# First branch of a two-layer block: scores with the queries on partitions, both directions in one weight map

## What is computed

```python
dmat = jnp.where(tril, b[..., :, None] - b[..., None, :] + ic[..., None, :], -jnp.inf)
a = jnp.exp(dmat - m_row[..., None]) * jnp.einsum('bhtd,bhsd->bhts', qc, kc)
num = jnp.einsum('bhts,bhsv->bhtv', a, vc) + ...
den = jnp.sum(a, axis=-1) + ...
h = num / jnp.maximum(jnp.abs(den), jnp.exp(-m_row))[..., None]
...
return h_lat[0] + h_lat[1], h_ctx[0] + h_ctx[1]      # forward + backward
...
hn = rmsnorm(h, a_norm_w)                            # then * sigmoid(o) * silu(z)
```

## Time and profile before

| what | value |
|---|---|
| median of 3 runs | 2305.05 us (2304.82 to 2305.26) |
| profiled execution, its own time | 2304.28 us |
| its span, first to last instruction | 2302.1 us |
| PE busy | 2278.4 us, 99% |
| DVE busy | 1335.7 us, 58% |
| ACT busy | 1066.3 us, 46% |
| granted TensorE clock, mean | 0.999 |
| DMA | 294.48 MB, mean 128 GB/s |

### The profile page before, as it was taken

One profiled execution on the slowest core, in us unless ns is written; L12 is line 12 of the kernel. 1 busy time (PEld: TensorE's weight loads), 2 busy tenths in 40 slices (PEclk: granted clock), 3 DMA queues, 4 the chain that ended last, 5 costly groups with the idle time before them and its releaser, 6 DMA issues.

```text
span 2302.1 us, 36859 instructions
## 1 busy us (share of the span) xinstructions
PE 2278.4 (99%) x15426; PEld 2033.1 (88%) x15426; DVE 1335.7 (58%) x2557; ACT 1066.3 (46%) x2064; POOL 237.6 (10%) x248
## 2 busy tenths in 40 slices
PE   8999999999999999999999999999999999999998
PEld 7888878999978998889999999999989888979887
DVE  6544443477754223456455676547667876667875
ACT  5533322355442223354443555445376554476553
POOL 0000000322201012100002221120100110100110
PEclk9999999999999999999999999999999999999999
DMA  7422224221234222233333223446524545323554
GB/s 305 170 75 75 74 110 183 93 74 56 74 108 147 75 74 88 86 130 109 110 129 131 108 77 108 176 140 218 165 93 141 189 168 192 133 82 139 190 178 144
DMA packets 52628, 294.48 MB, mean 128 GB/s; under 512 B 9008, under 2 KB 15408, under 8 KB 21168
## 3 DMA queue, kind: packets, MB, share of 16 engines
q1 hardware_dynamic: 52464, 292.15, 35.4%
HBM read 288.98 MB, written 3.41 MB: 127 GB/s over the span
## 4 chain that ended last, share of the span: by engine, by line
PE 93%; DVE 4%; ACT 2%; DMA 0%; issue 0%; SPq 0%; DVEq 0%; ACTq 0%
PE PS L583 90%; PE PS L587 3%; DVE TM L2339 1%; ACT TM L1625 1%; ACT TMG L1625 1%; DVE wl L2358 0%; DMA raw<-in_wpk 0%; DVE colS L2347 0%; DVE colS L2892 0%; DVE TMG L2347 0%; DVE wl L2360 0%; DVE HY L2347 0%; DVE TM L2508 0%; ACT HY L1625 0%; DVE TM L2347 0%
## 5 line engine op out<-in xcount | busy, mean ns | idle before, releaser
L583 PE MATMUL PS<-HY,wh 128*128 128x512 f32 (+3 forms) x4944 | 1278.1, 342 | 3.4 <-DVE HY L2347 1.0
L583 PEld LDWEIGHTS PS<-HY,wh 128*128 128x128 f32 (+2 forms) x4944 | 848.2, 189 | 115.6 <-issue 4.1
L583 PE MATMUL PS<-HY,wl 128*128 128x256 f32 (+1 forms) x3000 | 926.1, 309 | 0.0
L2358 DVE TENSOR_TENSOR wl<-raw,wh 128x1280 fp32r<-128x1280 f32 (+3 forms) x241 | 350.5, 1454 | 429.0 <-ACT wh L1635 428.8
L583 PEld LDWEIGHTS PS<-HY,wl 128*128 128x128 f32 x3000 | 567.4, 189 | 30.0
L583 PE MATMUL PS<-wh,HY 128*128 128x256 f32 x2916 | 551.7, 286 | 0.2
L583 PEld LDWEIGHTS PS<-wh,HY 128*128 128x128 f32 x2916 | 461.8, 191 | 3.4 <-ACT TM L1625 1.6
L1625 ACT ACTIVATE TM<-PS 128x512 f32<-128x512 f32 (+5 forms) x383 | 190.1, 510 | 584.1 <-PE PS L583 473.8
L583 PE MATMUL PS<-wl,HY 128*128 128x256 f32 x1458 | 412.5, 283 | 0.0
L1635 ACT ACTIVATE wh<-raw 128x1280 fp32r<-128x1280 f32 (+2 forms) x247 | 297.1, 1203 | 217.5 <-PE PS L583 138.7
L583 PEld LDWEIGHTS PS<-wl,HY 128*128 128x128 f32 x1458 | 279.4, 192 | 0.4
(11 more groups left out here) (190 smaller groups left out, 1693.1 us busy)
## 6 DMA issues: line engine op xcount, KB each, us to landing
raw<-in_wpk SPq DMA_DIRECT2D x233, 1024.0 KB, 4.8
raw<-in_wpk SPq DMA_DIRECT2D x32, 704.0 KB, 4.0
TM<-in_wpk SPq DMA_DIRECT2D x6, 1024.0 KB, 16.3
X<-in_xin SPq DMA_DIRECT2D x1, 2048.0 KB, 15.7
Y<-in_wpk SPq DMA_DIRECT2D x2, 1024.0 KB, 20.4
Y<-bias_d SPq DMA_DIRECT2D x4, 512.0 KB, 10.3
raw<-in_wpk SPq DMA_DIRECT2D x3, 512.0 KB, 3.7
T<-in_tabs SPq DMA_DIRECT2D x1, 1216.0 KB, 5.5
```

The source lines that it names most:

```text
L583: return P.x.matmul(o, l, r, start=start, stop=stop)
L2358: D.x.tensor_tensor(wl[:, s, 0:c], raw[:, r, 0:c], wh[:, s, 0:c], ALU.subtract).then_inc(*lo_split.mark((u, 0)))
```

## The change

The scores are computed with the queries on partitions. DVE multiplies scores and weights and sums each row in the same instruction (`tensor_tensor_reduce`), so the column of ones goes. The denominators of all tiles and both directions are worked out together, each direction's map is scaled by its reciprocal, and both are added into one map `a_w`. PE turns this map with transposes (`turns`), ACT copies it to SBUF (`a_wt`, in the buffer `Y`), and PE multiplies it by the values once (`outs`). ACT squares and scales straight from PSUM. Where these steps stand: for heads 1 to 3 `turns` is between the two passes of `a_z`; for head 0 of layer 0 it is after them; for head 0 of layer 1 the next head's queries (`queries(1)`) come first. `used("a_o")` on ACT and DVE moves ahead of the exponentials and products in head 0, and behind `a_w` on DVE in the others.

```diff
+        a_valid = ({i: (0, 128 * i + 128) for i in range(4)}, {0: (0, 256), 1: (128, 256), 2: (0, 512), 3: (0, 512)})
+        a_masks = (mb, mf)
+        a_diagonals = [TM[:, o:o + 2560].rearrange("p (i c) -> p i c", c=640)[:, :, 0:128] for o in (2052, 4100)]
+        a_w = (a_b[:, 0, 0:256], a_f[:, 1, 0:256], a_b[:, 2], a_f[:, 3])
+        a_den = colS[:, 8:16].rearrange("p (d i) -> p d i", d=2)
...
+        def a_turn_bank(i):
+
+            return bank(4)[:, 256 * i:256 * i + 256] if i < 2 else bank(4 + i)
...
+        def a_out_bank(l, i):
+
+            if l:
+                return bank(i)[:, 0:256]
+            return bank(2 + i // 2)[:, 256 * (i % 2):256 * (i % 2) + 256]
...
+                def turns(h):
+                    for i in range(i0, 4):
+                        P.wait_ge(dve_step, ("a_w", l, h, i))
+                        for k in range(0, a_keys(i), 128):
+                            t = turned(a_turn_bank(i)[:, k:k + 128], a_w[i][:, k:k + 128])
+                        if i:
+                            t.then_inc(*pe_step.mark(("a_turned", l, h, i)))
+
+                def outs(h):
+                    P.wait_ge(act_step, ("a_v", l, h, 1))
+                    for i in range(i0, 4):
+                        P.wait_ge(act_step, ("a_wt", l, h, i))
+                        last = a_keys(i) // 128 - 1
+                        for j in range(last + 1):
+                            t = mm(a_out_bank(l, i), a_wt(i)[:, 128 * j:128 * j + 128], a_v[:, j], j == 0, j == last)
+                        if l:
+                            t.then_inc(*pe_step.mark(("a_out", l, h, i)))
+                        elif i % 2:
+                            t.then_inc(*pe_step.mark(("a_out", l, h, i - 1), ("a_out", l, h, i)))
...
                     if h:
-                        P.wait_ge(dve_step, ("a_h", l, h - 1, 3))
+                        P.wait_ge(act_step, ("a_hn", l, h - 1))
                     for d in range(2):
-                        t = mm(bank(2 + d)[:, t0:512], ident[dirs[d], 32 * d + h:32 * d + h + 1].to_broadcast([4, 128]), a_r[d][:, t0:512])
+                        t = mm(bank(2 + d), ident[dirs[d], 32 * d + h:32 * d + h + 1].to_broadcast([4, 128]), a_c[d])
...
+                    for i in range(i0, 4):
+                        n = a_keys(i)
+                        mm(bank(4 + i)[:, 0:n], a_qk[:, 0, 128 * i:128 * i + 128], a_qk[:, 1, 0:n]).then_inc(
+                            *pe_step.mark(("a_s", l, h, i)))
...
+                        if h and c == 0:
+                            turns(h)
+                    if h:
+                        outs(h)
+                        if h < 3:
+                            queries(h + 1)
+                            keys(h + 1)
+                    elif l == 0:
+                        turns(0)
+                        queries(1)
+                        outs(0)
+                        keys(1)
+                    else:
+                        queries(1)
+                        turns(0)
+                        keys(1)
+                        outs(0)
...
+                def turned_weights(h):
...
+                    if l == 0:
+                        A.wait_ge(pe_step, ("a_turned", l, h, 1))
+                        act(Yf[:, 0:512], bank(4), ACT.Copy, ("a_wt", l, h, 0), ("a_wt", l, h, 1))
+                    for i in range(2, 4):
+                        A.wait_ge(pe_step, ("a_turned", l, h, i))
+                        act(a_wt(i), a_turn_bank(i), ACT.Copy, ("a_wt", l, h, i))
+
+                def squares_of(h):
+                    if h:
+                        A.wait_ge(pe_step, ("a_yt", l, h - 1, 1))
+                    for i in range(t0 // 128, 4):
+                        A.wait_ge(pe_step, ("a_out", l, h, i))
+                        act(a_h[:, i], a_out_bank(l, i), ACT.Square, ("a_sq", l, h), scale=0.5, accum_out=colS[:, 24 + i:25 + i])
...
+                    A.wait_ge(dve_step, ("a_root", l, h))
+                    for i in range(t0 // 128, 4):
+                        act(a_h[:, i], a_out_bank(l, i), ACT.Copy, ("a_hn", l, h), scale=colS[:, 28 + i:29 + i])
+
                 for h in range(4):
+                    if h == 0:
+                        used("a_o", 4 * l)
...
+                        x = a_diagonals[d][:, t0 // 128:4]
+                        act(x, x, ACT.Exp, *[("a_ex", l, h, d, i) for i in range(t0 // 128, 4)])
...
-                    used("a_o", 4 * l + h)
+                        used("a_o", 4 * l + h)
...
+                        if h and c == 0:
+                            turned_weights(h)
+                    if h:
+                        used("a_z", 4 * l + h)
+                        squares_of(h)
+                        scaled(h)
+                        if h < 3:
+                            queries(h + 1)
+                            keys(h + 1)
+                    elif l == 0:
+                        turned_weights(0)
+                        used("a_z", 0)
+                        queries(1)
+                        squares_of(0)
+                        scaled(0)
+                        keys(1)
+                    else:
+                        used("a_z", 4)
+                        queries(1)
+                        turned_weights(0)
+                        keys(1)
+                        squares_of(0)
+                        scaled(0)
...
-                        D.wait_ge(pe_step, ("a_out", l, h - 1, 3))
+                        D.wait_ge(pe_step, ("a_turned", l, h - 1, 3))
...
-                    for j in range(4):
-                        D.wait_ge(pe_step, ("a_s", l, h, j))
-                        for d in range(2):
-                            for a, z in a_valid[d][j]:
-                                a = max(a, t0)
-                                if z > a:
-                                    D.wait_ge(act_step, ("a_ex", l, h, d, j))
-                                    tt(a_dirs[d][:, j, a:z], bank(4 + j)[:, a:z], a_dirs[d][:, j, a:z], ALU.mult, ("a_at", l, h))
-                    used("a_o", 4 * l + h)
+                    if h == 0:
+                        used("a_o", 4 * l)
+                    for d in range(2):
+                        for i in range(i0, 4):
+                            a, z = a_valid[d][i]
+                            D.wait_ge(pe_step, ("a_s", l, h, i))
+                            D.wait_ge(act_step, ("a_ex", l, h, d, i))
+                            D.x.tensor_tensor_reduce(out=a_dirs[d][:, i, a:z], in0=bank(4 + i)[:, a:z], in1=a_dirs[d][:, i, a:z], scale=1.0,
...
+                    den = a_den[:, :, i0:4]
+                    D.wait_own(dve_step)
+                    stt(den, den, -1.0, den, ALU.mult, ALU.max)
+                    D.wait_own(dve_step)
+                    tt(den, den, a_cm.rearrange("p (d i) h -> p d i h", d=2)[:, :, i0:4, h], ALU.max)
+                    D.wait_own(dve_step)
+                    D.x.reciprocal(den, den).then_inc(*dve_step.mark())
+                    D.wait_own(dve_step)
+                    for i in range(i0, 4):
+                        d = 1 - i % 2
+                        ts(a_w[i], a_w[i], a_den[:, d, i:i + 1], None, ALU.mult, None)
+                    D.wait_own(dve_step)
+                    for i in range(i0, 4):
+                        d = i % 2
+                        a, z = a_valid[d][i]
+                        stt(a_w[i][:, a:z], a_dirs[d][:, i, a:z], a_den[:, d, i:i + 1], a_w[i][:, a:z], ALU.mult, ALU.add, ("a_w", l, h, i))
+                    if h:
+                        used("a_o", 4 * l + h)
...
-                    for i in range(i0, 4):
-                        den = colS[:, 8 + 2 * i:10 + 2 * i]
-                        D.wait_ge(pe_step, ("a_out", l, h, i))
-                        cp(den, a_banks(l, i)[:, :, 256])
...
-                        D.wait_ge(act_step, ("a_hf", l, h, i))
-                        D.wait_own(dve_step)
-                        stt(a_h[:, i], a_banks(l, i)[:, 1, 0:256], den[:, 1:2], a_h[:, i], ALU.mult, ALU.add, ("a_h", l, h, i))
```

More of the change, by code:

```diff
@@ L381, in program @@
         a_zero = [a_z[p, 1] for p in dirs]
-        a_r = [rows[p] for p in dirs]
+        a_c = [rows[p] for p in dirs]
         a_m = [a_g[p, 0] for p in dirs]
-        a_c = [a_rr[p, 1] for p in dirs]
+        a_r = [a_rr[p, 1] for p in dirs]
         a_bs = [a_rr[p, 0] for p in dirs]
@@ L759, in first_units, with queries @@
                             chunk(bank(1), uq, 128, k - lag, 0, 512, ("a_k", l, 0), ("unit", uq))
-                def qk_unit(h):
+                def queries(h):
                     u = place["a_qk", 4 * l + h]
@@ L764, in qk_unit, with keys @@
                     proj_t(bank(0)[:, 0:N], u, 0, 128, H, ready, 0, 8, t0, N, ("a_q", l, h))
+                def keys(h):
+                    u = place["a_qk", 4 * l + h]
                     P.wait_ge(dve_step, ("a_z", l, h - 1, 1))
@@ L872, in value @@
                     elif br == "a":
```

(10 more changed lines are left out.)

92 lines of the change are left out of this document (28 added, 64 removed).

## The result

| | us |
|---|---|
| changed kernel, median of 4 runs | 2292.86 (2292.69 to 2293.68) |
| before, same job, median of 4 | 2305.16 (2304.82 to 2305.30) |
| ratio, 95% interval | 0.9946 (0.9934 to 0.9959) |
| profiled execution, own time / span | 2293.68 / 2291.9 |

The change is 12.3 us faster; 7.6 were forecast. In a second job with five runs the same kernel came to 2293.29 (2292.88 to 2294.01) against 2303.08, ratio 0.9957 (0.9944 to 0.9971), 9.8 us. So the changed kernel is where it was, the kernel before came out 2 us lower, and the difference is 10 to 12. In the first job of the experiments three executions took 5504, 6073 and 9890 us, two of the kernel before and one of e5_warm, and every median and range here leaves them out.

The account below looks back on a forecast made before the run. PE, busy 99% of the span, was taken to bound the kernel. 13.2 us saved less 5.6 of waits gave 7.6 off 2304.28, 2296.7, and with the median 0.77 above, 2297.5 us; 8-in-10 range 2294 to 2303.

Parts of the forecast that it names:

- What bounds the kernel: Whole kernel: PE is busy 99% of the span, so time is its instruction count plus whatever makes it stand still.
- PE's saving: Branch on PE: 2.09 us a head in layer 0, 1.20 in layer 1, together 13.2 us less.
- The row sum: Read behind each DVE product: 0.2 us each, 0.8 us a head in layer 1, 1.6 in layer 0.
- the lower of the two bounds: DVE's row sum costs nothing; the upper bound was a scan, 1.21 us over 512 columns.
- The rest of the chain: DVE ahead of `turns`, layer 1: denominators 0.7 us, scaling two maps 0.9, adding maps 1.3 to 1.4.
- The waits: PE stands 3.2 us in layer 1 head 0, 1.2 each in heads 2 and 3; 5.6 given back.
- The clock: Behind the 3 us stall of layer 1, head 0, PE's clock may fall, costing 1.6 us.
- The sum: 13.2 us saved less 5.6 given back: 7.6 us, a median of 2297.5 us.
- the cheap bound: No cost for the row sum gives 0.8 us back at three places: 2295.1 us.
- Nothing waits: Rival: row sum costs little, the chains fit, 2 to 3 us of stall remain; 2294 to 2295 us; 8%.
- The three slower ones: Rivals: row sum like a scan, 2306 us, 13%; pair over 0.8 us above a product, 5%; unseen wait, about 2302, 12%.
- wait at another place: Rival: an unseen wait (late `a_z` step, ACT's order in head 0) takes half the gain; about 2302 us; 12%.

Follow-up runs that it names:

- e5_warm: Changed kernel with 18 matmuls of unused result filling the idle stretch ahead of the queries' pass in layer 1, head 0; 2294.01 us.
- e9: Changed kernel with every transpose of a map made twice into the same bank; 2301.69 us.
- e10: Changed kernel with every product of the turned maps with the values made twice; 2329.15 us.
- e3_no_sum: Changed kernel with plain products and no row sums, denominators computed from a constant; 2293.42 us.
- e6_memory_late: Changed kernel with the squares of the memory moved behind the merged maps on DVE in layer 1, heads 2 and 3; 2292.30 us.
- e4_sum_apart: Changed kernel with plain products and the row sums taken behind them by separate reductions on DVE; 2304.86 us.
- e2_layer0_order: Changed kernel with the maps turned ahead of the queries' pass in layer 1, head 0 (transposes, queries, values, keys); 2291.47 us.
- e7_both: Changed kernel with half 0's `a_z` step ahead of the denominators in layer 1, head 0, and the memory squares behind the merged maps; 2288.78 us.
- e5b_warm10: Changed kernel with 10 matmuls of unused result filling the idle stretch ahead of the queries' pass in layer 1, head 0; 2290.90 us.

## Where the prediction was right and where wrong

**What bounds the kernel: right.** PE's busy time fell by 13.1 us, the slow pass of head 0 included, and each PE record that was added or doubled came back in full (e9, e10), but for 0.2 us in head 2 of layer 1, where a wait stood.

**PE's saving: right, a little small.** Layer 0 gained 2.17 us a head for 2.09: the value products take 4.99 us (120.00 to 124.99) for 5.10. Layer 1 gained 1.35 for 1.20, seen in head 1, which waits for nothing. Most of that is again the value products, 3.26 us (1088.97 to 1092.23) for 3.37. The two scores of 512 columns take 1.42 us (1074.77 to 1076.19) and not 1.67, but this is no gain: the pair of records behind them takes 0.63 us where it took 0.42 before. Together 14.1 for 13.2.

**The row sum: the step that failed.** "I take 0.2 for the read, because the product no longer overlaps with what follows: 0.8 us a head in layer 1". It does overlap: the four sums cost 0.03 us (e3_no_sum), and the lower of the two bounds held. The term was 0.77 us too large in each head of layer 1, and it makes up about 2.0 of the 2.5 us by which the waits below were put too high. The rest of the chain stood well: counted from the head's start, the unit ahead of the products ends at 5.56 us, as forecast; denominators 0.62 for 0.7, scaling 0.91 for 0.9, the sum of the maps 1.20 for 1.3.

**The waits: places right, sizes too large.** Head 0 waited 2.18 us for 3.2 and heads 2 and 3 0.46 for 1.2 (39.54 against 39.08 in e6_memory_late), head 1 and layer 0 not at all. 3.1 us for 5.6. Of the 1.0 us in head 0, 0.65 is the row sum and 0.13 smaller terms. The other 0.2 is in PE's arrival, which the prediction put 8.80 us after the head's start. PE could have gone on 8.84 after it, but the listed wait begins only at 9.00, the end of the last record. In heads 2 and 3 the shorter chain on DVE left the first map 0.18 us late and the second 0.28.

**The clock: named, and left out of the sum.** The prediction had "after the 3 us stall the clock may fall", 1.6 us, for the range only. It fell, for 1.5 us.

**The sum.** 7.6 forecast; plus 0.9 (saving), plus 2.5 (waits), less 1.5 (clock) is 9.5, and the heads give 9.4. So the mechanism was right, and the branch was 1.8 us better than forecast. From there the range was missed by what is no part of the branch. With the branch as it came out and the rest as forecast the time would have been 2295.7, inside the range. The prediction put the median 0.77 us above the profiled execution, as it was before; after, it lies 0.82 below. And the profiled executions are 10.6 us apart in their own times, 1.2 more than the branch. Of that, 0.4 is start and end, 0.36 stands ahead of the first head of layer 0, 0.58 between the branches of the two layers, and 0.15 came back behind them. Those 2.8 us were in no term, and the low end of the range stood 1.1 us under the 2295.1 of the cheap bound, with nothing for either. No run shows why; the last section shows single executions drifting by about 2 us.

**The rivals.** "Nothing waits" had named a cheap row sum with 2 to 3 us of stall left, and got 8%. It was nearly the case, 3.1 us, though its 2294 to 2295 is above what was measured as well. The three slower ones fell: the pair costs 0.01 us more than the plain product, and there was no wait at another place. The half rate that the Trainium skill names (Vector Engine (DVE) Microarchitecture Reference, Points that are easy to get wrong) for two sources in SBUF that are not bf16 had no case in the pair, as one of its sources is PSUM; no run here shows a pair with both in SBUF. The plain sum of the two maps, both in SBUF, took 1.28 us for 384 and 512 columns (1045.72), where two products of the same widths with one source in PSUM take 1.15 (1041.77 to 1042.24, and 0.68), so it did not run at half rate.

## What to carry to other kernels

When an operation that the trace doesn't have is bounded by nothing and by something, look at whether it can run beside its neighbour before pricing it as a step of its own: a small read behind a long operation was free here, a reduction of its own over the same data cost as much as the product. When a chain on one engine grows, list what is queued behind it that it doesn't feed: the `a_z` step needed nothing of the maps, stood behind them, and cost 3.9 us. Price a stall on TensorE as the stall plus the slow pass that can follow it, and compare edits of a microsecond by the length of a repeated stage in the trace, not by the median.

## What the runs showed of the hardware

**The clock after equal stalls.** In e4_sum_apart PE idled 4.49, 2.34 and 2.34 us in heads 0, 2 and 3. The stretches behind them, the passes in the main:

```profile
1050.24:1054.58 4.34, 4.34 (x25) 4.34 (x26) 3.24 (x4) 0.00 (x0) 0.00 (x0) 0.64 0.08 9
1130.90:1133.70 2.80, 2.80 (x26) 2.80 (x25) 2.07 (x3) 0.75 (x2) 0.00 (x0) 1.00 0.04 6
1172.70:1177.10 4.40, 4.40 (x27) 4.40 (x25) 2.13 (x3) 0.81 (x2) 0.00 (x0) 0.61 0.32 88
```

After the same 2.34 us the clock held in head 2 and fell in head 3; twice as long a stall cost no slower a pass. In heads 2 and 3 the eight transposes stood between the stall and the pass, at a clock of 1.00 in both. And after 1.19 us of idle time the clock held (e2_layer0_order). So the slow pass is a cost that may follow a stall, about 1.5 us whether the stall is 2.18 or 4.49, and the stall's length does not settle whether it comes.

**Matmul spacing drifts in two late stretches.** Number of matmul records that PE completed in 50 us without idling, the same work at a granted clock of 1.00. The columns are stretch, us, PE busy, PEclk, DMA share, GB/s. The kernel before:

```profile
900.00:950.00 50.00, 50.00 (x222) 1.00 0.23 84
1800.00:1850.00 50.00, 50.00 (x285) 1.00 0.52 184
2140.00:2190.00 50.00, 50.00 (x290) 1.00 0.53 190
```

The changed kernel:

```profile
900.00:950.00 50.00, 50.00 (x222) 1.00 0.27 99
1800.00:1850.00 50.00, 50.00 (x291) 1.00 0.54 190
2140.00:2190.00 50.00, 50.00 (x285) 1.00 0.53 189
```

And e7_both, which is as before again:

```profile
1800.00:1850.00 50.00, 50.00 (x285) 1.00 0.55 189
2140.00:2190.00 50.00, 50.00 (x290) 1.00 0.54 190
```

At 900 us each of the thirteen profiles has 222 or 223. At 1800 and at 2140 it is 285 in one execution and 289 to 291 in another, 2% apart, in every combination and whatever the edit: e6_memory_late has 285 in both stretches, e5b_warm10 290 and 291. The DMA share there is twice that at 900, but it doesn't tell the two rates apart: at 1800 it is 0.52 in the kernel before with 285 records and 0.52 in e5b_warm10 with 290. The profiled executions of before and after are 10.33 us apart at the wait ahead of the first stretch (1694.01 and 1683.68), 12.23 behind it (2013.86 and 2001.63), and 10.18 at the last matmul. So one stretch moves the time by about 2 us, which is the size by which the medians of the kernel before differ between jobs. No run looked for the cause. That it stands where the DMA share is high is only seen, not shown.
